# The modulation projection of a two-block transformer: whole fp32 blocks stationary, two vectors moving, in an unrolled program

## What is computed

```python
mod_lat = silu(c) @ w_mod + b_mod          # w_mod: 2048 x 12288, 96 MB
mod_ctx = silu(c_ctx) @ w_mod + b_mod
sh1, sc1, gt1, sh2, sc2, gt2 = split(mod_lat, 6);  csh1, csc1, ... = split(mod_ctx, 6)
h_ctx = rmsnorm(ctx, g1) * (1 + csc1) + csh1
h     = rmsnorm(x + pos, g1) * (1 + sc1) + sh1
parts, parts_ctx = h @ w_in, h_ctx @ w_in  # q, k, v, gate, 2 x 16 decay ranks, Fourier input, gates
# chunked gated linear attention over ctx, then over x, forward and backward;
# 2-D DFT of the Fourier input; x += gt1 * merge(...) @ w_out
# x += gt2 * (relu(h2 @ w_mlp_in) ** 2) @ w_mlp_out
```

## Time and profile before

| | us |
|---|---|
| median of 3 runs | 3168.16 |
| the runs | 3168.16, 3155.83, 3168.32 |
| span of the profiled execution, first to last instruction | 3159.7 |
| PE busy | 2888.4 (91%) |
| PE weight loads busy (PEld) | 2640.5 (84%) |
| DVE busy | 1734.0 (55%) |
| ACT busy | 1345.7 (43%) |
| granted TensorE clock, mean | 0.961 |

### The profile page before, as it was taken

The page is one execution under the profiler, slowest core; times in us unless marked ns, Lnnn a source line. Parts: engine busy times, 40 slices in busy tenths (PEclk is TensorE's granted clock), DMA queues, the critical chain, the costliest instruction groups (busy, mean ns, idle before and its releaser), DMA issues.

```text
span 3159.7 us, 49860 instructions
## 1 busy us (share of the span) xinstructions
PE 2888.4 (91%) x21239; PEld 2640.5 (84%) x21239; DVE 1734.0 (55%) x1928; ACT 1345.7 (43%) x1455; POOL 5.5 (0%) x13
## 2 busy tenths in 40 slices
PE   5899989899999989999999996984969999999997
PEld 3378844468999989999999996984969999999996
DVE  3842477754444445455444544597456654664664
ACT  4642376543444354343343434332344444443442
POOL 0000000000000000000000000000000000000000
PEclk9999999999999999999999998997989999999998
DMA  8823477654555535555555552542425554555542
GB/s 299 317 74 106 137 248 251 213 186 154 180 184 186 201 124 186 174 177 186 171 187 166 182 187 80 171 135 93 147 67 188 186 187 165 182 182 192 182 165 81
DMA packets 271305, 543.50 MB, mean 172 GB/s; under 512 B 10697, under 2 KB 13693, under 8 KB 269981
## 3 DMA queue, kind: packets, MB, share of 16 engines
q1 hardware_dynamic: 269580, 529.20, 49.9%
q10 hardware_dynamic: 832, 6.39, 0.5%
q0 software_dynamic: 720, 5.31, 0.4%
HBM read 536.67 MB, written 4.19 MB: 171 GB/s over the span
## 4 chain that ended last, share of the span: by engine, by line
PE 81%; DVE 8%; ACT 4%; issue 4%; DMA 2%; SPq 1%; DVEq 0%; ACTq 0%
PE acc L265 22%; PE acc L269 22%; PE acc L267 22%; DVE wlo L228 3%; PE mp L421 2%; PE acc L371 2%; ACT whi L212 2%; PE acc L375 2%; PE acc L373 2%; DMA raw<-in_w_mod 1%; DVE cacc L1132 1%; PE acc L286 1%; PE acc L287 1%; PE mp L375 1%; PE mp L373 1%
## 5 line engine op out<-in xcount | busy, mean ns | idle before, releaser
L228 DVE TENSOR_TENSOR wlo<-raw,whi 128x1024 fp32r<-128x1024 f32 (+1 forms) x1016 | 1216.6, 1213 | 1158.8 <-ACT whi L212 1148.0
L212 ACT ACTIVATE whi<-raw 128x1024 fp32r<-128x1024 f32 (+1 forms) x1016 | 1048.8, 1049 | 1479.1 <-PE acc L269 1188.9
L265 PE MATMUL acc<-hh,whi 128*128 128x256 f32 x3616 | 1037.7, 287 | 69.0 <-DVE hl L457 24.2
L269 PE MATMUL acc<-hh,wlo 128*128 128x256 f32 x3616 | 1032.0, 285 | 0.6 <-issue 0.6
L267 PE MATMUL acc<-hl,whi 128*128 128x256 f32 x3616 | 1032.5, 286 | 0.0
L265 PEld LDWEIGHTS acc<-hh,whi 128*128 128x128 f32 x3616 | 703.3, 195 | 78.5 <-issue 61.9
L267 PEld LDWEIGHTS acc<-hl,whi 128*128 128x128 f32 x3616 | 703.6, 195 | 0.0
L269 PEld LDWEIGHTS acc<-hh,wlo 128*128 128x128 f32 x3616 | 703.1, 194 | 0.0
L265 PE MATMUL acc<-mh,whi 128*128 128x256 f32 x2240 | 628.4, 281 | 21.4 <-DVE ml L1218 15.4
L269 PE MATMUL acc<-mh,wlo 128*128 128x256 f32 x2240 | 629.0, 281 | 0.0
L267 PE MATMUL acc<-ml,whi 128*128 128x256 f32 x2240 | 625.8, 279 | 0.0
(11 more groups left out here) (229 smaller groups left out, 1915.0 us busy)
## 6 DMA issues: line engine op xcount, KB each, us to landing
raw<-in_w_mod SPq DMA_DIRECT2D x96, 1024.0 KB, 5.2
raw<-in_w_in SPq DMA_DIRECT2D x96, 1024.0 KB, 5.2
raw<-in_w_up SPq DMA_DIRECT2D x88, 1024.0 KB, 5.0
raw<-in_w_mlp_in SPq DMA_DIRECT2D x64, 1024.0 KB, 5.1
raw<-in_w_mlp_out SPq DMA_DIRECT2D x64, 1024.0 KB, 5.0
raw<-in_w_down SPq DMA_DIRECT2D x44, 1024.0 KB, 5.0
raw<-in_w_out SPq DMA_DIRECT2D x32, 1024.0 KB, 5.0
raw<-in_w_fourier_out SPq DMA_DIRECT2D x8, 1024.0 KB, 4.9
```

What stands on the lines that cost most here:

```text
L212: nc.scalar.activation(whi[:, r, :, 0:width], raw[:, s, 2 * j:2 * j + 2, 0:width], ACT.Copy).then_inc(hi_done[s], 1)
L228: nc.vector.tensor_tensor(wlo[:, r, :, 0:width], raw[:, s, 2 * j:2 * j + 2, 0:width], whi[:, r, :, 0:width].bitcast(f32), ALU.subtract).th ...
L265: nc.tensor.matmul(dst, whi[:, r, k, cols], hi[:, kt, :], start=begin, stop=False, skip_group_check=True)
L269: last = nc.tensor.matmul(dst, wlo[:, r, k, cols], hi[:, kt, :], start=False, stop=kt == first + 4 * len(which) - 1, skip_group_check=True)
```

## The change

Kernel after, in its parts:

- `load` takes a slot as one contiguous 128x2048 block (8 KB per partition); the host lays all weights out so. w_mod slots are freed by PE (`mod_used`), the others by DVE.
- w_mod isn't split. For each slot, 16 fp32 matmuls with a 128x128 block of `raw` stationary and the two vectors, `cv[:, kt, 0:2]`, moving; the result is already in columns. `mrow`, `mod_turn` and the conversions of w_mod go away.
- Ticks are whole slots, 64 of them in the scans, and on PE only.
- x, ctx and the parameters come transposed from the host; the position table comes as two factors. The order of the first 8 groups is 0, 4, 1, 5, 2, 6, 3, 7, so that a quarter of the modulation is applied after each pair. The sums of the first norms stand between slots of groups 1 and 2.
- The 32 rank columns get a slot of 64 columns of their own (`mm_lr`: weights stationary, 256 tokens moving, x and ctx); the other six token groups are whole. `L1368` and the copy of `lrT` go away.
- All `Fori` loops are Python loops.

```diff
-        def mod_piece(pe, st, i, s, j):
...
+        def mod_slot(pe, st, i, s):
+            if s == 0 and st.f[i]:
                 pe.wait_ge(acc_free[i], st.f[i])
+            k = MSLOT[st.m]
+            slot_in(pe, k)
             for t in range(4):
-                last = nc.tensor.matmul(acc[i][:, GC + 2 * t:GC + 2 * t + 2], mrow[:, t * P:(t + 1) * P], pair_w,
-                                        start=True, stop=True)
-            last.then_inc(S["mT_ps"], 1)
+                for c in range(4):
+                    last = nc.tensor.matmul(acc[i][:, 2 * c:2 * c + 2],
+                                            raw[:, k % NSLOT, t * GC + c * P:t * GC + (c + 1) * P],
+                                            cv[:, 4 * s + t, 0:2], start=s + t + c == 0, stop=s + t == 6,
+                                            skip_group_check=True)
+            last.then_inc(S["mod_used"], 1)
...
+        def mm_lr(pe, st, i):
+            pe.wait_ge(acc_free[i], st.f[i])
+            r = st.p % 4
+            pe.wait_ge(S["lo_n"], st.p + 1)
+            for kt in range(KT):
+                cols = slice(kt * LRW, (kt + 1) * LRW)
+                for x, (hi, lo) in enumerate(((hh, hl), (ch, cl))):
+                    dst = acc[i][0:LRW, x * GC:x * GC + NT]
+                    nc.tensor.matmul(dst, whi[:, r, cols], hi[:, kt, :], start=kt == 0, stop=False)
+                    nc.tensor.matmul(dst, whi[:, r, cols], lo[:, kt, :], start=False, stop=False)
+                    last = nc.tensor.matmul(dst, wlo[:, r, cols], hi[:, kt, :], start=False, stop=kt == KT - 1)
...
-        T_LR, T_Z, T_CUM, T_QK, T_SC, T_STATE, T_FFT, T_ONORM = 2, (3, 3), (2, 3), 2, 2, 2, 2, 4
+        T_Z, T_CUM, T_QK, T_SC, T_STATE, T_FFT = (2, 3), (1, 2), 1, 1, 1, 1
+        assert 4 * (sum(T_Z) + sum(T_CUM) + T_QK + T_SC + 4 * T_STATE + 2 * T_FFT) == NMOD[1]
...
+            nc.gpsimd.memset(cv[:, :, :], 0.0).then_inc(S["cz_ok"], 1)
...
+            act.dma_start(par[:, 0:2 * KT], ins["par"][:, 0:2 * KT]).then_inc(S["c_in"], 16)
...
+            act.dma_start(xT[:, :, :].rearrange("p t n -> p (t n)"), ins["xT"]).then_inc(S["x_in"], 16)
...
+            for n in range(8):
                 for s in range(4):
+                    mod_slot(pe, st, n % 2, s)
+                    if n in (1, 2):
+                        norm_quad(pe, n - 1, mp[n - 1], s)
...
             for g in range(FGROUPS):
...
-            mod_row(dve, st, 0)
-            mod_out(dve, 23, 0)
+            mod_out(dve, 23, 1)
+            C(4, met=0)
...
-            with pe.Fori(0, MLP_CHUNKS) as c:
-                it = st.inside(c, 8, (2, 2))
+            for c in range(0, MLP_CHUNKS):
                 for g in range(4):
-                    mm_feature(pe, it, g % 2, hh, hl, 0, ready=h_ready(pe, 8),
+                    mm_feature(pe, st, g % 2, hh, hl, 0, ready=h_ready(pe, 8),
```

More of the change, by code:

```diff
@@ L181, in build @@
         block = ctx.enter_context(nc.Block())
[L184 to L205, removed]
-            if j == 0:
[L207 to L215, removed]
@@ L217, in conv_lo, with load @@
-        def conv_lo(dve, st, slots, width=GC, behind=None):
-            for s, j, _ in pieces(slots):
-                lo_piece(dve, st, s, j, width)
+        def load(sp, st, name, slot, n=4, cols=4 * GC):
+            for i in range(slot, slot + n):
+                if st.k >= NSLOT:
+                    c = STREAM[st.k - NSLOT]
+                    before = STREAM[:st.k - NSLOT + 1]
+                    if c == "m":
+                        sp.wait_ge(S["mod_used"], before.count("m"))
+                    else:
+                        sp.wait_ge(S["lo_n"], 2 * before.count("d") + before.count("l"))
+                s = st.k % NSLOT
+                sp.dma_start(raw[:, s, 0:cols], ins[name][i]).then_inc(raw_full[s], 16)
+                st.k += 1
@@ new lines, in lo_piece, with conv_hi @@
+        def lo_piece(dve, st):
+            k, j = PIECE[st.p]
+            r, s = st.p % 4, k % NSLOT
+            dve.wait_ge(S["hi_n"], st.p + 1)
+            nc.vector.tensor_tensor(wlo[:, r, :], raw[:, s, 2 * GC * j:2 * GC * (j + 1)],
+                                    whi[:, r, :].bitcast(f32), ALU.subtract).then_inc(S["lo_n"], 1)
+            st.p += 1
+        def conv_hi(act, st, n=8, met=None):
+            st.e += n if met is None else met
+            for _ in range(min(n, len(PIECE) - st.p)):
+                hi_piece(act, st)
@@ L221, in conv_lo @@
+        def conv_lo(dve, st, n=8, met=None, behind=None):
+            st.e += n if met is None else met
+            for _ in range(min(n, len(PIECE) - st.p)):
+                lo_piece(dve, st)
                 if behind:
                     behind()
[L224 to L248, removed]
+        def group_done(eng, st):
+            eng.wait_ge(S["used"], st.e)
@@ L249, in mm_feature @@
+        def mm_feature(pe, st, i, hi, lo, frees, nkt=KT, w=GC, ready=None, free=None, stop=True):
             if free:
                 pe.wait_ge(*free)
-            else:
+            elif st.f[i]:
                 pe.wait_ge(acc_free[i], st.f[i])
[L253 to L273, removed]
@@ L295, in mod_turn @@
[L295 to L313 removed]
+            per = 2 * GC // w
@@ L387, in build @@
+            st.f[i] += 2 if with_ctx else 1
+        MOD_ORDER = (0, 4, 1, 5, 2, 6, 3, 7) + tuple(range(8, 24))
+        TOKEN = [(C_K, True), (C_V, True), (C_V + GC, True), (C_LR, True), (C_Q, False), (C_U, False),
+                 (C_U + GC, False)]
+        F_TOKEN = [4 + sum(2 if cw and c0 != C_LR else 1 for n, (c0, cw) in enumerate(TOKEN) if n % 2 == i)
+                   for i in range(2)]
         F_MOD = [f + 8 for f in F_TOKEN]
@@ L473, in apply_act @@
                     part = tmp[:, n % 2, t * NT:(t + 1) * NT]
-                    last = nc.scalar.activation(part, part, ACT.Identity,
+                    last = nc.scalar.activation(part, part if src is None else src[:, kt, :], ACT.Identity,
                                                 bias=shift(kt) if shift else 0.0, scale=scale(kt))
@@ L544, in _ @@
-            with sp.Fori(0, 2) as c:
-                ffn(st.inside(c, 12, (0, 0)), c, 4, 4)
-            st.passed(2, 12, (0, 0))
-            ffn(st, 2, 3, 3)
+            st = Turn()
+            for g in MOD_ORDER[:8]:
+                load(sp, st, "w_mod", 4 * g)
+            load(sp, st, "w_in", 0, 12)
+            load(sp, st, "w_lr_in", 0, 1, cols=2 * GC)
+            load(sp, st, "w_in", 12, 12)
+            for g in MOD_ORDER[8:]:
+                load(sp, st, "w_mod", 4 * g)
+            load(sp, st, "w_in", 24, 8)
@@ new lines, in _ @@
+            for j in range(4):
+                load(sp, st, "w_in", 32 + 4 * j)
+                load(sp, st, "w_in", 48 + 4 * j)
+                load(sp, st, "w_fourier_out", 2 * j, 2)
+                load(sp, st, "w_gla_out", 2 * j, 2)
+            load(sp, st, "w_out", 0, 16)
+            for c in range(MLP_CHUNKS):
+                load(sp, st, "w_mlp_in", 16 * c, 16)
+                for g in range(4):
+                    load(sp, st, "w_mlp_out", 16 * g + 4 * c)
+            load(sp, st, "w_in_2", 0, 34)
@@ new lines, in _, with first @@
+            last.then_inc(S["xt_sb"], 1)
+            def first(q):
+                for v in range(2):
+                    part = mpre[:, v, 1, 4 * q:4 * q + 4]
+                    last = nc.vector.scalar_tensor_tensor(part, part, 1.0, pcol("norm1_g", 4 * q, 4),
+                                                          ALU.add, ALU.mult)
+                last.then_inc(S["ma_ok"], 1)
+                for v, (hi, lo) in enumerate(((hh, hl), (ch, cl))):
+                    apply_lo(dve, 2 * q + v, hi, lo, q)
@@ L909, in _ @@
+            mod_out(dve, 7, 1)
+            C(4, met=0)
+            for i in range(2):
+                dve.wait_ge(acc_free[i], 4)
+            first(3)
+            dve.wait_ge(S["lo_ok"], 8)
+            nc.vector.memset(lrT[:, :], 1.0).then_inc(S["lr_one"], 1)
+            for n, (c0, cw) in enumerate(TOKEN):
+                if c0 == C_LR:
+                    C(1)
+                    continue
+                C(4 if n == 6 else 8, met=8)
                 group_done(dve, st)
```

777 lines of the change are left out of this document (315 added, 462 removed).

## The result

The changed kernel takes **3473.14 us** (median of 4 runs, 3470.3 to 3485.39) against 3166.41 (3155.83 to 3168.32): ratio 1.0984, 95% interval 1.0959 to 1.1009. It is slower by a tenth, as forecast (3489, range 3380 to 3580). The profiled execution has a span of 3483.6 us, 323.9 above the one of before.

A forecast was written before the change was run, and what follows sets the result against it. Transfers bound the start before; the prediction had PE bind it instead, with long w_mod runs at the low clock. 90-16+274-27 = +321 gave span 3481; with 8.5 us carried over to the median, 3489 us, range 3380 to 3580.

The forecast's parts named there:

- Step 1: Start to the first token matmul: 32 w_mod slots at the low clock plus norm sums, ending at 254 us, +90 us.
- Step 2: Token stage: 32-column rank matmuls go, 96 mm_lr matmuls of 256 columns come, -16 us.
- Step 3: Scans and Fourier: 64 w_mod slots, 16 at the high clock and 48 at the low one, +274 us.
- Step 4: Unrolled loops: PE's four jump-back gaps and the low clock after them go, 6.9 us each, -27 us.
- Step 5: Contiguous loads, contiguous constants and host layouts in the split matmuls after the scans; convolution taps keep their work: 0 us.
- A: Rival for start and scans: the high clock holds under the new w_mod matmuls; -26 us in all, 3142 us, chance 12%.
- B: Rival: only the start loses the clock, in the scans other matmuls keep it; +90 us, 3258 us, chance 6%.
- C: Rival: low clock throughout the scans, dense bursts included; in all +404 us, 3572 us, chance 8%.
- D: Rival: unrolling starves the instruction fetch, so the loops' 27 us are not won; 3516 us, chance 1%.

The follow-up runs named there:

- Experiment 1: The changed kernel with each w_mod matmul moving 128 columns instead of 2, the two vectors repeated by a stride of 0: 3135.31 us.
- experiment 4: The changed kernel with 128 moving columns per w_mod matmul in the first 8 groups only, 2 in the ticks: 3366.55 us.
- experiment 5: The kernel before with only TensorE's two large MLP loops written out: 3137.22 us against 3164.76 for the kernel before beside it.
- experiments 2 to 4: The changed kernel moving 64 (3290.09 us) or 32 columns (3453.43); 64 with 128 in the first group (3261.78); 128 in the start only (3366.55).

## Why the prediction was right

*The clock.* The whole forecast hung on one row group, the 16 us of 32-column matmuls in the earlier trace rows, and it carried over: 1007 of 1024 records in the start at 0.213. Experiment 1 shows that this price is the clock's: the same loads, in the same number, at 0.112. One thing differs from the row that the forecast leaned on: there the high clock was lost, in the start it was never won. By the Trainium skill's rule ("TensorE: Matmul & The Clock Gate", Part 1), busy without gaps is enough; here PE was busy 245.88 of 245.88 us with a pitch of 0.213, so for matmuls that stream two columns the measurement decides against it. The price of a weight load on the same page of the Trainium skill (LDWEIGHTS), columns/1.2, holds at the high clock only (0.112 against 0.107) and not at the low one (0.213).

*Step 1*, forecast +90, measured +92.5. First matmul at 9.4 (9), w_mod and the norm sums until 255.28 (254), and a wait of 1.48 us for the first `wlo` of the tokens that I had left out. The same wait ahead of L265, at the end of the scans, had been charged. (The 27 us for the norm sums are 28 by their own working, 64 x 0.44, within the rounding.)

*Step 2*, -16, measured -15.9.

*Step 3*, +274, measured +283.2. Of the two terms that were low by 5 to 6 us each, one is the number of slots that keep the high clock behind dense work: 16 assumed, about 460 of 2048 records measured, 14.4 slots' worth. With that the w_mod records take 462 x 0.112 + 1586 x 0.213 = 390 us (384 forecast); the other is the rest of PE's 577, 187 (182). The waits came to 3.9 us (6). The "16 matmuls of 512 columns" of a w_mod slot in the kernel before are 8 (`mod_piece` issues 4 for half a slot); no term rests on it. That the errors are small is partly luck: experiment 4 has 10 us less for the same scans, and at 64 columns the same work varied by 28.

*Step 4*, -27: 28 in the two traces, 27.5 alone in experiment 5.

*Step 5*, priced at 0, was wrong by 6 us. "The stage of the convolution taps keeps its work" held for VectorE's arithmetic, but not for its order: half-size pieces and waits on ScalarE stood in front of the taps, where VectorE is the bound, and they are gone with the host's packing (read from the traces, not tried alone).

*The sum*, 3481 on the profiled span against 3483.6; the terms that were off, +2.5, +9 and -9, cancel. The rest of the distance between 3489 and 3473 is a term taken over from before: there the median lay 8.5 us above the profiled span, here it lies 10.5 below, 19 us that have no part in the mechanism.

*The rivals.* A is false for two columns; with 128 (experiment 1) its times come out. B, only the start loses the clock, is false: the scans took 580.9 us, and in experiment 4 they lost it with the start at the high clock. C, low clock throughout, is nearer than B; it failed by the 460 or so records at the high clock, and the time is 99 us under its 3572. D is excluded by 732.59 busy of 732.89 us in straight code.

## What to carry to other kernels

A matmul with few moving columns costs its weight load at the granted clock, and here that clock stayed low through 246 us of unbroken work: before making a wide operand stationary under a thin one, price the load at both clocks. If the thin operand must move, let it move 128 columns by a stride of 0, which here took back 338 us for a few edited lines; better, make it stationary in strips of 32 columns side by side: that kernel, with the unrolled loops and layouts of the changed one, is 4.6% under the kernel before. Read the pitch of the matmuls where a window lies ahead of the trace's first clock record.

## What the runs showed of the hardware

- A 128x128 fp32 weight load followed by few columns goes on at 0.112 or 0.213 us by the granted clock; run without any idle time it had the low clock at 2 and 32 moving columns (246 and 191 us) and the high one at 128.
- At 64 columns both occur in one kernel (0.216 at 9 us, 0.112 for 640 records from 84 us on): the clock stayed high behind denser matmuls and fell after waits of 2.30 and 2.44 us. Runs of one such kernel differ by 28 us.
- In the scans, once lost, the low clock lasted from 472.4 to 684.0 us in one piece, through dense bursts of 2 to 4 us. The kernels of experiments 2 to 4 lost it at the same place, right behind the token stage, and for the same 211.6 us; with 128 columns it was 3.4 us. In each of the five kernels the low stretch ended at the same work, the first scan step on x, where two fp32 matmuls of 512 columns come together (four records, 3.7 us here) instead of one:

```profile
680.58 2.05 PE L1219 MATMUL mp<-lab,con 128*128 128x512 f32 x2
682.43 1.82 PE L1221 MATMUL mp<-lab,con 128*128 128x512 f32 x2
```

- Four column strips of an fp32 matmul run side by side: 8 records of 512 columns in 1.06 us at the high and 1.87 at the low clock, where two that run in turn start 0.43 apart at the high one.
- A jump back of TensorE's large loops cost 7 us: 4.2 of waiting and the low clock behind it.
